# A hybrid conv and gated-linear-attention block: the transposes of the normalized x made by the DMA queue

## The chip, the cores and the metric

The kernel runs on the 8 cores of one Trainium2 chip. Each core has 4,096 of the 32,768 tokens (two of the 16 sequences of 2,048) and does the same work on them; the cores don't speak to each other. The metric is the device time of the slowest core in microseconds (us), as the median of several runs.

## The reference, cut to what matters

x is (16, 2048, 1024) in float32. One layer is computed:

```python
h = rms_norm(x, norm_g)
proj = h @ w_in                      # 1024 -> 8208 columns
c_val, c_gate, c_z, q, k, v, g_lr, g_r, m_conv, m_gla = split(proj)
y_conv = conformer_conv_branch(c_val, c_gate, c_z, ...)   # GLU, 31 taps over positions, LayerNorm, two silu, @ w_conv_out
log_a = log_sigmoid(g_lr @ gate_w2 + gate_b) / 16
o = gla_chunked(q, k, v, log_a)      # causal gated linear attention, 4 heads
y_gla = (rms_norm(o) * silu(g_r)) @ w_gla_out
y = sigmoid(m_conv) * y_conv + sigmoid(m_gla) * y_gla
out = rms_norm(x + y @ w_out)
```

What the change touches is h: every projection multiplies the transpose of h, so h, computed with tokens on the partitions, has to be turned so that its 1,024 channels lie on the partitions.

## The kernel before, in words

**Tiles.** A core's tokens are cut into 8 tiles of 512 (t = 0 to 7), and a tile into 4 slices of 128 tokens (s = 0 to 3). `tile(t)` (line 833) runs the stages of one tile: the GLU units, v, the convolution, q and k, the gates, the attention with the z and m projections as filler, and then an end stage: a loop over c = 0 to 7 (line 940) of three weight units each (g_wco line 916, g_mg line 923, g_wgo line 930), and `wout` (line 792). A unit is a block of 128 x 1024 weights and 8 matmuls of 128x512 on TensorE, 1.73 us.

**The normalized x.** In the end stage of tile t the x of tile t + 1 is made ready, slice by slice. `pre_load` (line 427) loads 128 tokens of x into xa, one of two buffers. `pre_elem` (line 433) squares and sums them on ScalarE (line 440, whose full output is thrown away into hb), takes the inverse root on GpSimd (lines 443 and 446) and writes the scaled slice in bf16 into hb on VectorE (line 449). hb too has two buffers, p = s % 2. `pre_pe` (line 454) transposes the slice: eight 128x128 transposes on TensorE (line 458) from hb into the PSUM bank pb6, and one ScalarE copy (line 461) from pb6 into hT, which holds the transposed tile and has two buffers (hbuf = t % 2). For tile 0 this runs ahead of the first tile, with x in U1. For the others the loop at line 940 calls pre_pe of slice c - 2 at c = 2 to 5, pre_elem of slice c at c = 0 to 3 right behind it, and pre_load of slices 2 and 3 at c = 0 and 1; slices 0 and 1 are loaded in the stage ahead (line 908). The first reader of the new hT is `gate_in(t + 1)` (line 578), at the start of `wout`; it waits for all four slices.

**The order.** Every operation is recorded by `S.op` (line 64) in program order, with the buffers that it reads and writes. Each engine runs its own list in that order; waits between engines come from the buffers, and an engine stands still at a wait with all that is behind it. A write to a buffer waits for the buffer's last write and for its readers. A DMA that SyncE (SP) issues counts as the reader or writer until it has landed. hT[hbuf] is one buffer for all four slices.

**The weights.** All weights pass through SBUF once for each tile. In the first three tiles they come in float32 (512 KB a unit, line 329) into one of 5 staging buffers, are cast to bf16 by VectorE or ScalarE in turn (lines 352 and 355), and a third of them is written back to the DRAM tensor w_b at a time (line 364): tile 0 takes all in float32, tile 1 two thirds, tile 2 one third. The rest, and everything from tile 3 on, is loaded in bf16 from w_b (256 KB a unit, line 345). `advance` (line 367) records these casts and loads ahead of each unit: casts for the next 4 units (LOOK), loads for as many as there are buffers for: 12 units until tile 3, then 22 (NX). All these DMAs are issued by SP, as are those of x, of the result and of the convolution's shifted rows.

Of the kernel before, what the change touches and what calls it, by code (L numbers as in the profile page):

```python
# [148 lines left out]
def build_nc(n_tiles=NT):  # L149
# [13 lines left out]
    S = Sched()  # L163
    dma_sem_names = []

    def newsem(name):
        dma_sem_names.append(name)
        return name

    with ExitStack() as es:  # L170
        def sb(name, shape, dt):
            return es.enter_context(nc.sbuf_tensor("sb_" + name, shape, dt))
# [17 lines left out]
        hb = sb("hb", [128, 2, D], BF16)  # L190
        hT = sb("hT", [128, 2, 8, T], BF16)
# [34 lines left out]
        B = {}  # L226
# [38 lines left out]
        def x0_load(s):  # L265
# [8 lines left out]
             dma_sem=newsem("c_gn"))  # L274
        for s_ in range(1, 4):
# [12 lines left out]
             reads=[B["scanm"]], writes=[B["scanm"]])  # L288
# [126 lines left out]
        def proj_from(t, uid, src, srcbufs, perk=False):  # L415
# [6 lines left out]
                    reads=[wbuf] + ([srcbufs[kc]] if perk else list(srcbufs)), writes=[PB[bi]])  # L422
            return bi

        xa_sems = [newsem("xa0"), newsem("xa1")]

        def pre_load(t, s):
# [26 lines left out]
        def pre_pe(t, s):  # L454
            p = s % 2
            hbuf = t % 2
            for c in range(8):
                S.op("pe", lambda e, p=p, c=c: e.transpose(
                    out=pb6[:, c * 128:(c + 1) * 128], in_=hb[:, p, c * 128:(c + 1) * 128], identity=identb[:]),
                    reads=[B["hb"][p], B["identb"]], writes=[PB[6]])  # L460
            S.op("act", lambda e, hbuf=hbuf, s=s: e.activation(
                out=hT[:, hbuf, :, s * 128:(s + 1) * 128],
                in_=pb6[:].rearrange("p (c t) -> p c t", c=8), func=AF.Copy),
                reads=[PB[6]], writes=[B["hT"][hbuf]])
# [368 lines left out]
        def tile(t):  # L833
# [106 lines left out]
            for c in range(8):  # L940
                g_wco(c)
                g_mg(c)
                if c == 0:
                    gla_c(t, 3)
                else:
                    g_wgo(c - 1)
                if more:
                    if 2 <= c < 6:
                        pre_pe(t + 1, c - 2)
                    if c < 4:  # L950
                        pre_elem(t + 1, c)
                    if c in (0, 1):
                        pre_load(t + 1, c + 2)
# [6 lines left out]
        for s_ in range(4):  # L960
            pre_elem(0, s_)
            if s_ > 0:
                pre_pe(0, s_ - 1)
        pre_pe(0, 3)
        set_pbanks([0, 1, 2, 3, 4, 5, 7])
        gate_in(0)
# [103 lines left out]
```

How the kernel before makes its waits and increments, by code:

```python
    def replay(self, eng, engobj, eng_sems, dma_sems):  # L135
        for o in self.prog[eng]:
            for k, v in o.waits:
                if k[0] == "e":
                    engobj.wait_ge(eng_sems[k[1]], self.cnts[k[1]][v])
                else:
                    engobj.wait_ge(dma_sems[k[1]], v)
            if o.fn is None:
                continue
            inst = o.fn(engobj)
            if o.dma_sem is not None:
                inst.then_inc(dma_sems[o.dma_sem], 16)
            elif o.marked:
                inst.then_inc(eng_sems[eng], 1)
```

## Time and profile before

| | |
|---|---|
| median of 3 runs | 1612.04 us (1610.75 to 1613.39) |
| the profiled execution | 1609.87 us |
| its span, slowest core (core 7) | 1608.3 us |
| spans of the 8 cores | 1592.6 to 1608.3 us |
| TensorE matmul busy | 1478.3 us, 92% |
| VectorE, ScalarE, GpSimd busy | 890.8, 705.4, 555.2 us |
| DMA engines busy with the main hardware queue | 71.5% of 16 engines' span |
| DMA traffic | 352.29 MB, mean 219 GB/s |

Times are those of core 7, from the first instruction to the last. PE is TensorE's matmul side, PEld its weight loads, DVE VectorE, ACT ScalarE, POOL GpSimd, SPq the DMA instructions that SyncE issues. L458 is line 458 of the kernel. In a row of grouped instructions "x8" counts them, and square brackets tell how long the engine had been idle before, and what it waited for. The granted clock (PEclk) is 1.00 at full speed.

### The profile page before, as it was taken

The page shows a single profiled execution, that of the slowest core. Times are in us where ns is not written, and L with a number is a line of the kernel's source. Part 1 is how long each engine was busy: PE and PEld are TensorE (multiplying, and loading weights), DVE is VectorE, ACT ScalarE, POOL GpSimd, SP SyncE. Part 2 cuts the span into 40 slices and gives each one's busy share as a digit, 9 for nine tenths or more (in the row PEclk, how much of TensorE's full clock was granted, in tenths as well). Part 3 has the DMA queues.
Part 4 walks back from the last instruction along what each step waited for, and adds up shares of the span by engine and source line. Part 5 has one row for each costly group of instructions (what it writes and reads, how often), then busy time and mean ns, then how long its engine had stood idle before and what let it go on. Part 6 is the DMA issues. An engine that isn't in the chain of part 4 may idle for free.

```text
span 1608.3 us, 28736 instructions; the slowest of 8 cores (1592.6 to 1608.3 us)
## 1 busy us (share of the span) xinstructions
PE 1478.3 (92%) x8960; PEld 703.2 (44%) x8960; DVE 890.8 (55%) x1259; ACT 705.4 (44%) x1184; POOL 555.2 (35%) x659
## 2 busy tenths in 40 slices
PE   4687989688999899999999999999999999999997
PEld 1233533234544345444554445444544445444553
DVE  3466645475545665476634665376644675366633
ACT  4235755226644256433644245233644246332631
POOL 1123223224223342254423452353423352352512
PEclk9898999889999999999999999999999999999999
DMA  6987899976899868898464955568564856568451
GB/s 184 292 235 222 274 314 318 291 231 200 269 322 286 255 205 252 268 268 243 153 220 143 247 177 184 177 192 242 151 223 145 229 188 200 178 180 241 134 175 53
DMA packets 174820, 352.29 MB, mean 219 GB/s; under 512 B 19536, under 2 KB 60624, under 8 KB 174672
## 3 DMA queue, kind: packets, MB, share of 16 engines
q1 hardware_dynamic: 174528, 350.32, 71.5%
q8 instruction: 76, 1.25, 0.3%
q14 instruction: 72, 0.59, 0.1%
q0 software_dynamic: 144, 0.13, 0.1%
HBM read 301.75 MB, written 48.76 MB: 218 GB/s over the span
## 4 chain that ended last, share of the span: by engine, by line
PE 73%; DMA 10%; DVE 7%; issue 4%; ACT 3%; SPq 2%; POOL 1%; DVEq 0%; POOLq 0%; ACTq 0%
PE ps_pb L409 33%; PE ps_pb L645 13%; PE ps_pb L419 11%; PE ps_pb L795 6%; PE ps_pb L507 4%; DMA sb_stg<-w 4%; DMA usc<-sb_u 3%; DVE sb_U L513 1%; DVE sb_FP L520 1%; SPq L498 1%; DMA w_b<-sb_wn 1%; ACT sb_wn L355 1%; PE ps_pb L707 1%; PE ps_pb L703 1%; PE ps_pb L712 1%
## 5 line engine op out<-in xcount | busy, mean ns | idle before, releaser
L409 PE MATMUL ps_pb<-sb_hT,sb_wn 128*128 128x512 bf16 x2152 | 492.7, 383 | 16.1 <-ACT sb_wn L355 6.9
L409 PEld LDWEIGHTS ps_pb<-sb_hT,sb_wn 128*128 128x128 bf16 x2152 | 209.8, 99 | 271.2 <-issue 38.2
L645 PE MATMUL ps_pb<-sb_wn,sb_hT 128*128 128x512 bf16 x768 | 191.6, 408 | 53.1 <-ACT sb_wn L355 33.1
L409 PE MATMUL ps_pb<-sb_hT,sb_stg 128*128 128x512 bf16 x920 | 207.0, 379 | 1.2 <-issue 0.8
L419 PE MATMUL ps_pb<-sb_big,sb_wn 128*128 128x512 bf16 x744 | 174.7, 382 | 0.4 <-DVE sb_wn L352 0.4
L936 POOL TENSOR_TENSOR sb_yb<-sb_FP 128x512 bf16<-128x512 f32 x64 | 82.7, 1293 | 213.0 <-DVE sb_FP L933 213.0
L645 PEld LDWEIGHTS ps_pb<-sb_wn,sb_hT 128*128 128x128 bf16 x768 | 77.6, 103 | 163.0 <-issue 87.0
L409 PEld LDWEIGHTS ps_pb<-sb_hT,sb_stg 128*128 128x128 bf16 x920 | 89.4, 98 | 105.4 <-issue 2.6
L355 ACT ACTIVATE sb_wn<-sb_stg 128x1024 bf16<-128x1024 f32 x88 | 92.3, 1050 | 98.3 <-DMA sb_stg<-w 98.1
L674 POOL TENSOR_SCALAR sb_Rbf<-sb_Tst,sb_gar 128x256 bf16<-128x256 f32 x128 | 65.7, 531 | 190.8 <-DVE sb_Tst L718 190.7
L522 POOL TENSOR_TENSOR sb_FP<-sb_FP,sb_yb 128x512 f32<-128x512 f32 x56 | 73.8, 1319 | 157.0 <-ACT sb_yb L516 157.0
L555 POOL TENSOR_TENSOR sb_U<-sb_U,sb_FP 128x512 f32<-128x512 f32 x64 | 97.1, 1544 | 57.3 <-DVE sb_FP L541 57.3
L419 PEld LDWEIGHTS ps_pb<-sb_big,sb_wn 128*128 128x128 bf16 x744 | 72.1, 99 | 83.7 <-issue 4.3
L352 DVE CAST sb_wn<-sb_stg 128x1024 bf16<-128x1024 f32 x89 | 68.5, 776 | 63.6 <-DMA sb_stg<-w 63.5
L926 ACT ACTIVATE sb_FP<-ps_pb 128x512 f32<-128x512 f32 x64 | 38.0, 594 | 137.0 <-PE ps_pb L409 116.9
L489 POOL COPY sb_halo<-sb_u 128x30 bf16<-128x30 bf16 x64 | 50.9, 796 | 127.4 <-DVE sb_u L486 127.4
L449 DVE SCALAR_TENSOR_TENSOR sb_hb<-sb_xa,sb_ssx,sb_Gn 128x1024 bf16<-128x1024 f32 x28 | 36.0, 1284 | 102.2 <-POOL sb_ssx L446 102.2
L481 ACT ACTIVATE sb_FP<-ps_pb 128x512 f32<-128x512 f32 x64 | 38.1, 595 | 121.2 <-PE ps_pb L409 80.1
L795 PE MATMUL ps_pb<-sb_wn,sb_yb 128*128 128x512 bf16 x384 | 86.5, 379 | 4.8 <-ACT sb_wn L355 1.8
L740 DVE SCALAR_TENSOR_TENSOR sb_big<-ps_pb,sb_sso,sb_sgr 128x256 bf16<-128x256 f32 x128 | 61.9, 483 | 45.5 <-POOL sb_sso L732 35.5
L507 PE MATMUL ps_pb<-sb_big,sb_wn 128*32 128x512 bf16 x1472 | 80.7, 379 | 2.6 <-issue 2.6
L558 DVE TENSOR_TENSOR sb_U<-sb_U,sb_FP 128x512 f32<-128x512 f32 x64 | 71.1, 1136 | 18.6 <-ACT sb_FP L551 18.6
(115 smaller groups left out, 2083.0 us busy)
## 6 DMA issues: line engine op xcount, KB each, us to landing
sb_stg<-w SPq DMA_DIRECT2D x177, 512.0 KB, 7.7
sb_wn<-w_b SPq DMA_DIRECT2D x329, 256.0 KB, 4.5
sb_stg<-w_b SPq DMA_DIRECT2D x198, 256.0 KB, 3.8
sb_big<-usc SPq DMA_DIRECT2D x256, 135.0 KB, 4.8
w_b<-sb_wn SPq DMA_DIRECT2D x88, 256.0 KB, 6.6
sb_U<-x SPq DMA_DIRECT2D x36, 512.0 KB, 6.6
out<-sb_U SPq DMA_DIRECT2D x32, 512.0 KB, 4.0
sb_xa<-x SPq DMA_DIRECT2D x28, 512.0 KB, 5.4
```

The costliest lines, as they stand in the source:

```text
L352: S.op("dve", lambda e: e.tensor_copy(out=wn[:, slot, :], in_=stg[:, i, :]), reads=[B["stg"][i]], writes=[B["wn"][slot]])
L355: S.op("act", lambda e: e.activation(out=wn[:, slot, :], in_=stg[:, i, :], func=AF.Copy), reads=[B["stg"][i]], writes=[B["wn"][slot]])
L409: S.op("pe", lambda e, bi=bi, kc=kc, wap=wap: e.matmul(pb[bi][:], lhsT=wap[:, kc * 128:(kc + 1) * 128], rhs=hT[:, hbuf, kc, :], start=(kc ...
L419: S.op("pe", lambda e, bi=bi, kc=kc, wap=wap: e.matmul(pb[bi][:], lhsT=wap[:, kc * 128:(kc + 1) * 128], rhs=src[:, kc, :], start=(kc == 0) ...
L507: S.op("pe", lambda e, cbk=cbk, j=j, b=b, c=c, wap=wap: e.matmul(pb[cbk][32 * b:32 * b + 32, :], lhsT=wap[:, b * 256 + j * 32:b * 256 + j ...
L522: S.op("pool", lambda e: e.tensor_tensor(out=FP[:, S2, :], in0=FP[:, S2, :], in1=sq, op=ALU.add), reads=[B["FP"][S2]] + sqbuf, writes=[B[" ...
L555: S.op("pool", lambda e, c=c: e.tensor_tensor(out=U1[:, c, :], in0=U1[:, c, :], in1=FP[:, MU, :], op=ALU.subtract), reads=[B["U1"][c], B[" ...
L558: S.op("dve", lambda e, c=c: e.tensor_tensor(out=U1[:, c, :], in0=U1[:, c, :], in1=FP[:, RS, :], op=ALU.mult), reads=[B["U1"][c], B["FP"][ ...
L645: S.op("pe", lambda e, bi=bi, kc=kc, s=s, wap=wap: e.matmul(pb[bi][:], lhsT=hT[:, hbuf, kc, s * 128:(s + 1) * 128], rhs=wap[:, (kc % 2) * ...
L674: S.op("pool", lambda e, p=p, h=h, s=s: e.tensor_scalar(out=Rbf[:, p, h, :], in0=Tst[:, h, :], scalar1=gar[:, h, s:s + 1], scalar2=1.0, op ...
L795: S.op("pe", lambda e: e.matmul(pb[bi][:], lhsT=yb[:, kc, s * 128:(s + 1) * 128], rhs=wap[:, (kc % 2) * 512:(kc % 2) * 512 + 512], start=( ...
L936: S.op("pool", lambda e, c=c, t1=t1, g2=g2: e.tensor_tensor(out=yb[:, c, :], in0=FP[:, t1, :], in1=FP[:, g2, :], op=ALU.add), reads=[B["FP ...
```

## The change

From the second tile on (t > 0), a slice is transposed by one DMA that SP issues from hb straight into hT. The eight transposes on TensorE, their PSUM bank and ScalarE's copy are left out for these slices. Tile 0 is as before. The two semaphores are one for each hb buffer. The DMA reads hb[p] and writes hT[hbuf] by the bookkeeping of `S.op`.

```diff
+        ht_sems = [newsem("ht0"), newsem("ht1")]
         xa_sems = [newsem("xa0"), newsem("xa1")]
...
         def pre_pe(t, s):
             p = s % 2
             hbuf = t % 2
+            if t > 0:
+                S.op("sp", lambda e: e.dma_start_transpose(out=hT[:, hbuf, :, s * 128:(s + 1) * 128], in_=hb[:, p, :]),
+                     reads=[B["hb"][p]], writes=[B["hT"][hbuf]], dma_sem=ht_sems[p])
+                return
             for c in range(8):
```

## Rows read from the trace of the kernel before

**Rows 1.** The page: busy time of the engines, granted clock and DMA by slices

```profile
PE 1478.3 (92%) x8960; PEld 703.2 (44%) x8960; DVE 890.8 (55%) x1259; ACT 705.4 (44%) x1184; POOL 555.2 (35%) x659
...
PEclk9898999889999999999999999999999999999999
DMA  6987899976899868898464955568564856568451
```

**Rows 2.** The page: the chain that ended last, by engine

```profile
PE 73%; DMA 10%; DVE 7%; issue 4%; ACT 3%; SPq 2%; POOL 1%; DVEq 0%; POOLq 0%; ACTq 0%
```

**Rows 3.** Busy time by stretches: span, PE, PEld, DVE, ACT, POOL, clock, DMA share, GB/s

```profile
200.00:600.00 400.00, 349.90 (x2045) 160.00 (x2044) 221.55 (x304) 184.72 (x278) 128.36 (x146) 0.94 0.87 270
600.00:1608.00 1008.00, 984.77 (x6051) 478.31 (x6049) 564.80 (x798) 425.00 (x758) 375.18 (x441) 1.00 0.64 195
195.00:300.00 105.00, 91.84 (x446) 41.03 (x446) 53.15 (x72) 50.48 (x67) 29.32 (x39) 0.98 0.98 310
300.00:340.00 40.00, 26.58 (x190) 10.87 (x194) 17.36 (x23) 10.28 (x12) 5.02 (x5) 0.74 0.98 280
340.00:400.00 60.00, 51.95 (x331) 23.17 (x324) 39.09 (x53) 30.23 (x48) 26.82 (x24) 0.89 0.63 209
420.00:480.00 60.00, 56.95 (x300) 26.76 (x298) 25.45 (x39) 30.37 (x48) 15.25 (x18) 0.97 1.00 321
640.00:676.00 36.00, 35.45 (x195) 16.75 (x193) 15.60 (x22) 13.37 (x19) 11.67 (x14) 1.00 0.94 309
```

**Rows 4.** Waits of PE before 640 us: what for, us in total, times, longest

```profile
PE ps_pb L645 <- ACT sb_wn L355: 33.1, 12, 5.4
PE ps_pb L458 <- DVE sb_hb L449: 18.0, 3, 15.1
PE ps_pb L645 <- DVE sb_wn L352: 16.5, 7, 7.6
```

**Rows 5.** Timeline of PE in the end stage of tile 6

```profile
1374.99 0.61 PE L458 MATMUL ps_pb<-sb_identb,sb_hb 128*128 128x128 bf16 x8
1375.44 1.89 PE L419 MATMUL ps_pb<-sb_big,sb_wn 128*128 128x512 bf16 x8
1377.17 1.89 PE L409 MATMUL ps_pb<-sb_hT,sb_wn 128*128 128x512 bf16 x8
...
1391.87 0.61 PE L458 MATMUL ps_pb<-sb_identb,sb_hb 128*128 128x128 bf16 x8
1392.32 1.89 PE L419 MATMUL ps_pb<-sb_big,sb_stg 128*128 128x512 bf16 x8
...
1404.89 0.61 PE L584 MATMUL ps_pb<-sb_hT,sb_wglr 128*32 128x512 bf16 x8 [0.32 <-issue]
```

**Rows 6.** All instructions of line 461, with who waited for them

```profile
L461 ACT ACTIVATE sb_hT<-ps_pb x32: 1005/1023/1024, 16.2 to 1392.6; 128x1024 bf16<-128x1024 bf16 x32
...
  PE ps_pb L458: 3.0, 1
```

**Rows 7.** Timeline of ScalarE, VectorE and SP in the end stage of tile 6

```profile
1376.62 1.05 ACT L440 ACTIVATE sb_hb<-sb_xa 128x1024 bf16<-128x1024 f32 x1
1378.92 1.28 DVE L449 SCALAR_TENSOR_TENSOR sb_hb<-sb_xa,sb_ssx,sb_Gn 128x1024 bf16<-128x1024 f32 x1 [2.87 <-POOL sb_ssx L446]
1380.12 0.68 DVE L919 SCALAR_TENSOR_TENSOR sb_FP<-sb_yb,ps_pb 128x512 f32<-128x512 bf16 x1
...
1374.93 0.33 SPq L430 DMA_DIRECT2D sb_xa<-x  x1
1375.31 8.05 SPq L345 DMA_DIRECT2D sb_wn<-w_b  x8
```

**Rows 8.** DMA issues in 1368 to 1405 us: KB each, median us to landing

```profile
sb_wn<-w_b SPq DMA_DIRECT2D x13, 256.0 KB, 5.1
sb_stg<-w_b SPq DMA_DIRECT2D x10, 256.0 KB, 2.7
```

**Rows 9.** Timeline of SP and ScalarE in the end stage of tile 1

```profile
442.02 0.33 SPq L430 DMA_DIRECT2D sb_xa<-x  x1
...
445.11 6.73 SPq L329 DMA_DIRECT2D sb_stg<-w  x2
451.89 0.50 SPq L364 DMA_DIRECT2D w_b<-sb_wn  x1
...
447.24 1.06 ACT L440 ACTIVATE sb_hb<-sb_xa 128x1024 bf16<-128x1024 f32 x1 [4.02 <-DMA sb_xa<-x]
448.20 0.19 ACT L440 ACTIVATION_READ_ACCUMULATOR sb_hb<-sb_xa 128x1 f32 x1
448.51 1.06 ACT L355 ACTIVATE sb_wn<-sb_stg 128x1024 bf16<-128x1024 f32 x1
```

**Rows 10.** DMA issues in 420 to 470 us

```profile
sb_stg<-w SPq DMA_DIRECT2D x17, 512.0 KB, 11.0
w_b<-sb_wn SPq DMA_DIRECT2D x8, 256.0 KB, 10.7
```

**Rows 11.** The page: the main DMA queue's packets, MB, share of 16 engines

```profile
q1 hardware_dynamic: 174528, 350.32, 71.5%
```

## The prediction

> **What bounds the kernel now.** I read the page first. TensorE is busy 92% of the span [rows 1] and makes 73% of the chain that ended last, DMA 10% [rows 2]. These are averages over two regimes, so I cut the span into stretches. From 600 us on PE is busy 984.8 of 1008 us at full clock, with DMA at 0.64; from 200 to 600 us it is busy 349.9 of 400, with DMA at 0.87 [rows 3]. Up to tile 2 the weights come in float32, and there DMA is the bound: 0.98 from 195 to 340 us and 1.00 from 420 to 480, just where the end stages of tiles 0 and 1, and their transposes, lie [rows 3]. PE pays with waits for casts, 33.1 us for ScalarE's and 16.5 for VectorE's [rows 4]; the clock drops too, to 0.74 in the stretch where PE is most idle [rows 3]. In the end stages from tile 2 on PE is the bound: its groups follow each other without a gap [rows 5]. So the change touches two kinds of places: two slow boundaries (from tile 0 to 1 and 1 to 2, 8 slices) bound by DMA and casts, and five boundaries (20 slices) bound by PE.
>
> **What it removes.** From one group of eight transposes to the next matmul is 1375.44 - 1374.99 = 0.45 us, though the group's row says 0.61, as matmuls overlap [rows 5]. The last slice's group is alike, 1392.32 - 1391.87 [rows 5]; all 28 slices make 12.6 us. In the five PE-bound boundaries nothing else stands beside them, so 20 x 0.45 = **9.0 us** come off. In the other two, TensorE's 3.6 us lie in front of waits for weights: I count nothing. ScalarE's copy, 1.02 us x 28 = 29 us [rows 6], is no gain of its own where ScalarE has room; PE waited for it once, 3.0 us [rows 6], in the first boundary. I leave that as a bonus inside the range.
>
> **What it adds, on the DMA engines.** The kernel has no transposing DMA, so I bound it. Low end: 256 KB at the queue's mean rate while busy, 350.32 MB / (0.715 x 1608.3 us) = 305 GB/s, 0.86 us on all 16 engines [rows 11]. High end: a 128x128 block of bf16 has source rows of 256 bytes; if each of the 1,024 is a packet and costs as much as the mean packet now, 0.715 x 16 x 1608.3 us / 174528 = 105 ns [rows 11], a slice costs 1,024 x 105 / 16 ns = 6.7 us. A small packet should cost less than one of 2 KB, so I stay near the low end, at twice it, 1.7 us. A boundary then adds 6.8 us of DMA work. At the slow boundaries, with a share of 0.98 to 1.00, it goes on the path whole; at the others it is hidden, with 0.64 used and 22 units of weights (38 us) loaded ahead. It can't be below nothing, since no transfer is removed.
>
> The Trainium skill disagrees with itself here, and no row shows the DMA's side. Its page Advanced Engine Details and Errata (X-Bar Transpose) says that transposing DMAs are as fast as regular ones, which is my low end; by that an estimate of the sum is some 5 us lower, 1620. Its page VectorE: DVE Perf Modes (The three transpose paths) speaks against the change: 1309 ns for a 128x128 block by DMA, 390 on TensorE. Eight blocks one after another would be, as an estimate, 10.5 us a slice, beyond my high end, and the result that of rival (D) or above. For TensorE the trace differs from that page, with 0.45 us for all eight in a row.
>
> **What it adds, in waits.** Three are new. (1) hb has two buffers, and ScalarE's square of slice 2 writes into the one that slice 0's DMA reads. It stands right behind the DMA in the program, so ScalarE stands still until that has landed; likewise slices 3 and 1. Before, it waited for 0.45 us of TensorE. (2) The four DMAs write one buffer, so SP stands at each until the last has landed, its weight loads behind it. (3) SP waits for hb, which is written two iterations earlier and is ready. The issue itself, 0.33 us for a plain DMA [rows 7], could take longer; one or two us of it on SP are covered by the loads ahead.
>
> In the PE-bound boundaries: SP reaches slice 0's DMA after three loads from 1375.31, at about 1376.4 [rows 7]; it lands L later. From the start of a square to hb it is now 1378.92 + 1.28 - 1376.62 = 3.6 us, and 0.7 more for the VectorE operation behind it that empties a bank [rows 7]. The seven PSUM banks come round after 7 x 1.73 = 12.1 us, for the unit that starts at 1375.44 at 1387.5 [rows 5]. So PE is not held if 1376.4 + L + 4.3 is below 1387.5, L below 6.8 us. Landings of 256 KB here are 2.7 and 5.1 us [rows 8]. The last slice lands at some 1397, and gate_in starts at 1404.9 now [rows 5]. I price both waits at nothing here; the cover is those 2 to 4 us.
>
> In the slow boundaries a DMA of 256 KB lands after 10.7 us [rows 10]. SP reaches slice 0's DMA between 445 and 452 us, so it lands at 456 to 463, and the square that ran at 447.24, with the cast at 448.51 behind it, comes 9 to 16 us later [rows 9]. Casts are recorded only 4 units (7 us) ahead, so PE runs dry for 2 to 9 us, and slice 1's DMA, issued only when slice 0's has landed, does it again. DMA works on meanwhile through its full staging buffers, so this is not added whole to its 6.8 us: between 6.8 (all covered) and 17 (6.8 and two stalls of 5) I take 10 for each boundary, **20 us** in all. The boundary from tile 2 to 3 has DMA at 0.94 [rows 3] but a third of the casts: I take 2 us.
>
> **Sum.** -9.0 + 20 + 2 = +13. Against the profiled execution's 1609.9 us that is 1623; its time lies 2.2 us under the median of the runs, 1612.0, so I forecast 1625 us. About 0.2% (3 us) can be told from no change.
>
> **Rivals.**
> (A) *Hidden everywhere, faster.* The DMAs cost little and land soon, the staging buffers ride over ScalarE's stop, and only the 9 us (at best 12.6 and the 3.0) remain: 1603 us. For it: slices 2 and 3 of x land late anyway, and ScalarE already stood 4.02 us there [rows 9]; DMA has room behind the stage, 0.63 from 340 to 400 us [rows 3]. Against it: 0.98 to 1.00 in between. Chance 0.30.
> (B) *It cancels.* The slow boundaries lose 4 to 5 us each, DMA work at the low end and a short stop: 1612. Chance 0.10.
> (C) *My forecast,* slower by ScalarE's stop behind the queued DMA in tiles 0 and 1: 1625, own range 1616 to 1650. Chance 0.48.
> (D) *Long transposes, much slower.* At the high end, 6.7 us each, the slow boundaries add 54 us of DMA; with landings of 10 us in the wide tiles PE is held 3 us at each of five: -9 + 54 + 15 = +60, and some more for the stops, about 1680. It decides from L above 6.8 us. Chance 0.10.
> (E) *Not what it says:* if elements went one by one, or the DMA were cut into many, SP or the queue would be blocked for far longer, beyond 1700. Chance 0.02; nothing in the profile bears on it.
>
> **Range and chances.** The range runs from the centre of (A) over (B) to the end of (C), 1603 to 1650, and leaves out (D), (E) and the better side of (A), about 0.2. Faster is (A), 0.30; same is (B), 0.10; slower are (C), (D) and (E), 0.60.
>
> **What would show it.** Line 458 has 32 transposes in place of 256, line 461 4 copies, both before tile 0; between units of the end stage from tile 3 on nothing, and each of these stages 1.8 us shorter. A DMA row of 28 with a landing: under 6.8 us in late tiles and near 10 in tiles 0 and 1. Line 440 waiting for that DMA (what reads hb), most in tiles 0 and 1, and PE's waits for ACT L355 above 33.1 us. SP waiting at the second to fourth of each four. I am wrong if the stretch up to 600 us is not longer, or if the wide tiles show gaps on PE in the end stage, or if gate_in waits for the DMA.

## The result, and the profile after

The changed kernel takes 1645.38 us (median) against 1612.04 before: ratio 1.0195, 95% interval 1.0147 to 1.0243. It is slower, by 33 us where 13 were forecast. In some executions, of most of these kernels, the cores of one die show a lower granted clock and the time is some per cent longer; the ratios are taken without them. The profiled execution of the changed kernel has a span of 1643.9 us on core 4, the slowest. The page, in the lines that answer to [rows 1], [rows 2] and [rows 11]:

```profile
PE 1469.4 (89%) x8608; PEld 693.2 (42%) x8736; DVE 890.1 (54%) x1259; ACT 677.5 (41%) x1156; POOL 555.5 (34%) x659
...
PE 67%; DMA 11%; DVE 8%; issue 5%; ACT 3%; SPq 3%; POOL 2%; DVEq 0%; POOLq 0%; ACTq 0%
...
q1 hardware_dynamic: 204096, 357.67, 73.1%
```

And all instructions of line 459, the new DMA: durations on SP in ns (least, median, most), who waited for them (us, times), and the time to landing:

```profile
L459 SPq DMA_TRANSPOSE sb_hT<-sb_hb x28: 1237/1239/6661, 220.9 to 1429.4; - x28
...
  ACT sb_hb L441: 103.9, 14
...
DMA to landing us min/median/max: 3.1/5.5/11.0
```

There are 28 transposing DMAs, as said. Each brings (204096 - 174528) / 28 = 1,056 packets: the source's 1,024 runs of 256 bytes and little else. The queue's busy time went from 0.715 x 1608.3 to 0.731 x 1643.9 us, 51.8 us more, 1.85 us a slice on all 16 engines (1.7 was taken). These are two single cores; by the medians of the 8 cores it is 1.5 us. ScalarE waited 103.9 us for them, in 14 waits, two at each of seven boundaries. PE waited for one at the start of gate_in, once and for 0.4 us.

The stretches, in the columns of [rows 3], the last two cut out of stalls in the end stages of tiles 0 and 1:

```profile
200.00:600.00 400.00, 320.29 (x1792) 142.22 (x1816) 202.53 (x279) 156.80 (x236) 111.74 (x130) 0.90 0.86 257
600.00:1641.00 1041.00, 1003.50 (x5944) 484.03 (x6033) 580.73 (x822) 424.85 (x771) 391.44 (x456) 0.99 0.67 199
220.00:240.00 20.00, 7.40 (x25) 2.85 (x26) 3.68 (x5) 3.02 (x5) 2.00 (x3) 0.66 0.70 176
460.00:480.00 20.00, 8.08 (x26) 2.91 (x25) 3.08 (x4) 2.58 (x4) 2.00 (x3) 0.66 0.74 216
```

From 200 to 600 us PE is busy 320 us in place of 350. In the stalls the DMA share is 0.70 and 0.74, where it was 0.97 and 1.00 in the same stretches before: SP issues no loads for 8.3 us of the first one, as it waits for the cast on VectorE. The granted clock is 0.66 on average there, so it was for a part at 1.2 GHz, the lower of its two levels (full speed is 2.4), after PE had been idle for some 12 us.

The best measure is the time from one gate_in to the next, read from the timeline of each core. Medians over the 8 cores, of the profiled executions; the first column holds the boundary from tile 0 to 1:

```
                               0>1    1>2    2>3    3>4    4>5    5>6    6>7
before                       223.3  220.4  201.6  182.5  182.5  182.5  182.5
the changed kernel           235.6  235.0  213.5  180.8  181.3  180.7  180.8
e1 four hb                   225.1  221.0  203.1  181.1  180.7  181.0  180.8
e2 square elsewhere          232.3  230.2  209.7  182.1  181.8  180.7  180.8
e3 plain copy                238.6  235.2  215.1  181.7  181.2  181.1  181.4
e4 from tile 4               223.5  220.5  202.6  180.8  180.9  180.9  180.7
e5 four hb, four hT          222.9  221.2  202.2  181.1  181.2  181.4  181.1
e6 one step earlier          221.8  222.5  203.5  180.7  180.7  180.7  180.8
e7 twice, late               220.4  218.3  201.5  187.7  188.2  187.2  188.8
e8 four hb, TensorE          219.9  218.8  201.4  182.5  182.5  182.5  182.5
e9 one step earlier, again   223.6  224.1  202.1  180.7  180.7  180.7  180.8
e10 four buffers, from 3     221.2  221.0  200.4  181.3  181.4  181.2  181.0
e11 twice, early             242.6  237.1  218.2  182.2  180.7  181.0  180.8
e12 second aside             230.3  227.8  208.4  182.6  180.7  181.0  180.8
```

The changed kernel loses 12.3, 14.6 and 11.9 us at the first three boundaries and gains 1.2 to 1.8 at each of the last four: +32.4. The first two columns scatter by 2 to 4 us between executions of the same code for these tiles, the last four hardly. The profiled executions of e1 (1622.0 us) and e12 (1640.2 us) lie above the medians of their runs.

The end stage of tile 0: ScalarE, VectorE, PE and SP.

```profile
219.39 1.06 ACT L355 ACTIVATE sb_wn<-sb_stg 128x1024 bf16<-128x1024 f32 x1 [4.42 <-DMA sb_stg<-w]
230.14 1.06 ACT L441 ACTIVATE sb_hb<-sb_xa 128x1024 bf16<-128x1024 f32 x1 [9.70 <-DMA sb_hT<-sb_hb]
231.11 0.19 ACT L441 ACTIVATION_READ_ACCUMULATOR sb_hb<-sb_xa 128x1 f32 x1
231.20 1.04 ACT L355 ACTIVATE sb_wn<-sb_stg 128x1024 bf16<-128x1024 f32 x1
...
232.46 1.28 DVE L450 SCALAR_TENSOR_TENSOR sb_hb<-sb_xa,sb_ssx,sb_Gn 128x1024 bf16<-128x1024 f32 x1 [15.19 <-POOL sb_ssx L447]
233.66 0.69 DVE L352 CAST sb_wn<-sb_stg 128x1024 bf16<-128x1024 f32 x1
...
220.59 1.89 PE L419 MATMUL ps_pb<-sb_big,sb_wn 128*128 128x512 bf16 x8 [1.89 <-ACT sb_wn L355]
234.49 3.57 PE L409 MATMUL ps_pb<-sb_hT,sb_wn 128*128 128x512 bf16 x8 [12.01 <-DVE sb_wn L352]
...
220.90 4.03 SPq L459 DMA_TRANSPOSE sb_hT<-sb_hb  x1
224.99 1.03 SPq L364 DMA_DIRECT2D w_b<-sb_wn  x1
```

SP issues slice 0's transpose at 220.90, behind a full queue (the share of the DMA engines was 1.0 from 205 to 225 us), and is held 4.03 us by it. The square of slice 2 starts at 230.14, after a wait of 9.70 us, with the cast of an odd unit behind it. PE stands 12.01 us, and not for ScalarE but for *VectorE's* cast of an even unit: VectorE stands in its own order at the scaling of slice 2 (line 450), which needs that square's sum, and its cast comes behind it at 233.66. PE's next unit takes 3.57 us in place of 1.89, at the lower clock. The waits of PE for casts before 640 us, after and then before, to be read beside [rows 4]:

```profile
PE ps_pb L650 <- ACT sb_wn L355: 29.9, 12, 5.1
PE ps_pb L409 <- DVE sb_wn L352: 24.3, 3, 12.0
PE ps_pb L409 <- ACT sb_wn L355: 17.1, 6, 4.3
PE ps_pb L650 <- DVE sb_wn L352: 14.9, 8, 5.5
...
PE ps_pb L409 <- ACT sb_wn L355: 6.9, 4, 2.6
PE ps_pb L409 <- DVE sb_wn L352: 4.9, 5, 2.1
```

The waits in the v and gate stages (line 650) are no longer than before; at line 409 they have grown from 4.9 and 6.9 us to 24.3 and 17.1.

The end stage of tile 6, against [rows 5] and [rows 7]:

```profile
1414.33 1.32 SPq L459 DMA_TRANSPOSE sb_hT<-sb_hb  x1
...
1420.14 1.06 ACT L441 ACTIVATE sb_hb<-sb_xa 128x1024 bf16<-128x1024 f32 x1 [8.31 <-DMA sb_hT<-sb_hb]
...
1419.50 1.89 PE L409 MATMUL ps_pb<-sb_hT,sb_stg 128*128 128x512 bf16 x8
1421.22 3.62 PE L419 MATMUL ps_pb<-sb_big,sb_stg 128*128 128x512 bf16 x15
1424.68 1.89 PE L409 MATMUL ps_pb<-sb_hT,sb_stg 128*128 128x512 bf16 x8
```

Here too ScalarE stands 8.31 us, but PE runs without a gap: issue to landing is 5.8 us, under the 6.8 of the prediction. There are no casts to be late.

### The profile page after: what moved, and what is told of

The parts are those of the page before. It is cut to its first block, busy times and chain, and to the rows that moved or that the text cites. A ratio compares the mean times of both kernels' runs of the same rounds, so it can differ in the third digit from the quotient of the medians.

```text
span 1643.9 us, 28159 instructions; the slowest of 8 cores (1629.1 to 1643.9 us)
## 1 busy us (share of the span) xinstructions
PE 1469.4 (89%) x8608; PEld 693.2 (42%) x8736; DVE 890.1 (54%) x1259; ACT 677.5 (41%) x1156; POOL 555.5 (34%) x659
## 3 DMA queue, kind: packets, MB, share of 16 engines
q1 hardware_dynamic: 204096, 357.67, 73.1%
## 4 chain that ended last, share of the span: by engine, by line
PE 67%; DMA 11%; DVE 8%; issue 5%; ACT 3%; SPq 3%; POOL 2%; DVEq 0%; POOLq 0%; ACTq 0%
PE ps_pb L409 29%; PE ps_pb L650 12%; PE ps_pb L419 10%; PE ps_pb L800 6%; DMA usc<-sb_u 4%; PE ps_pb L512 4%; DMA sb_stg<-w 3%; DMA sb_hT<-sb_hb 3%; DVE sb_U L518 2%; DVE sb_FP L525 2%; SPq L503 1%; DMA w_b<-sb_wn 1%; ACT sb_wn L355 1%; DVE sb_wn L352 1%; DVE sb_HP L532 1%
## 5 line engine op out<-in xcount | busy, mean ns | idle before, releaser
L409 PE MATMUL ps_pb<-sb_hT,sb_wn 128*128 128x512 bf16 x2096 | 485.2, 385 | 48.8 <-DVE sb_wn L352 24.3
L650 PE MATMUL ps_pb<-sb_wn,sb_hT 128*128 128x512 bf16 x756 | 196.1, 416 | 51.0 <-ACT sb_wn L355 29.9
L409 PE MATMUL ps_pb<-sb_hT,sb_stg 128*128 128x512 bf16 x896 | 203.0, 379 | 2.8 <-ACT sb_yb L521 1.7
```

The costliest lines, as they stand in the source:

```text
L409: S.op("pe", lambda e, bi=bi, kc=kc, wap=wap: e.matmul(pb[bi][:], lhsT=wap[:, kc * 128:(kc + 1) * 128], rhs=hT[:, hbuf, kc, :], start=(kc ...
L650: S.op("pe", lambda e, bi=bi, kc=kc, s=s, wap=wap: e.matmul(pb[bi][:], lhsT=hT[:, hbuf, kc, s * 128:(s + 1) * 128], rhs=wap[:, (kc % 2) * ...
```

## The experiments

**Theory W**: the loss is a wait of a buffer's next writer for its reader. Slices 2 and 3 reuse the two hb buffers, and ScalarE and VectorE, which carry the casts, stop behind a DMA that is itself behind a full queue. **Theory Q**: the loss is the work of the DMA engines and of SP. All ratios are to the kernel before.

**e1: four buffers for hb.** Two are hb, two lie in HP, a tile that is idle then.

```diff
+        def hslot(s):
+            if s < 2:
+                return hb[:, s, :], [B["hb"][s]]
+            return (HP[:, 2 * s - 4:2 * s - 2, :].rearrange("p a t -> p (a t)"), B["HP"][2 * s - 4:2 * s - 2])
...
-                out=hb[:, p, :], in_=xs, func=AF.Square, accum_out=ssx[:, col:col + 1]),
+                out=hv, in_=xs, func=AF.Square, accum_out=ssx[:, col:col + 1]),
```

> The changed kernel with four buffers for the normalized slice (two of them in HP, which is idle there), so that neither ScalarE's square nor VectorE's scaling of slices 2 and 3 waits for a DMA transpose. Nothing is left out. Theory W (the loss is the stop of ScalarE and VectorE behind a transpose that is still in the queue): the 40 us of PE waits in the first three boundaries (12.0 + 4.3, 11.9 + 3.4, 4.3 + 4.5) vanish, and 1645 falls to between 1603 (the 9 us saved on PE, and the DMA work hidden) and 1618 (1.85 us of DMA work for each of 8 slices on the path). Theory Q (the loss is DMA and SP time: 1.85 us on 16 engines and 1.2 to 6.7 us of a held SP for each slice): still above 1635, with the same waits of PE for casts.

Measured: 1608.8 us, ratio 0.9967 (0.9936 to 0.9999). It is in W's range. On core 0, the same place as above; line 447 is the square, line 466 the transpose:

```profile
219.79 3.63 SPq L466 DMA_TRANSPOSE sb_hT<-sb_hb  x1
...
218.27 1.06 ACT L355 ACTIVATE sb_wn<-sb_stg 128x1024 bf16<-128x1024 f32 x1 [4.56 <-DMA sb_stg<-w]
219.24 1.04 ACT L447 ACTIVATE sb_HP<-sb_xa 128x1024 bf16<-128x1024 f32 x1
...
223.57 1.89 PE L409 MATMUL ps_pb<-sb_hT,sb_wn 128*128 128x512 bf16 x8 [0.70 <-DVE sb_wn L352]
...
PE ps_pb L596 <- DMA sb_hT<-sb_HP: 4.9, 3, 3.5
```

The same DMA, issued in the same way and holding SP for 3.63 us, costs PE almost nothing here: the square runs at once, and PE's 12.01 us are 0.70. All waits of PE for casts come to 61 us before, 98 in the changed kernel and 60 here (medians of the 8 cores). The three boundaries are 1.8, 0.6 and 1.5 us over those before, with all the DMA work still there. A new wait shows in the last line: gate_in (line 596) stands for the last transposes, 2.6 to 6.6 us in all on each core. That is about the size of what is left over.

**e2: only ScalarE freed.** The square's output, which nobody reads, goes elsewhere.

```diff
-                out=hb[:, p, :], in_=xs, func=AF.Square, accum_out=ssx[:, col:col + 1]),
+                out=HP[:, 0:2, :].rearrange("p a t -> p (a t)"), in_=xs, func=AF.Square, accum_out=ssx[:, col:col + 1]),
```

> The changed kernel, with the full output of ScalarE's square, which nobody reads, written into HP in place of hb. ScalarE no longer waits for a transpose; VectorE's scaling of slices 2 and 3 still does. Nothing of the result is left out. Theory W with ScalarE as the engine that matters: most of the 33 us go, 1615 to 1625. Theory W with either engine enough (VectorE carries half of the casts, and it stands at the same buffer): PE waits for VectorE's casts instead, 1635 to 1645. Theory Q: no difference, 1645.

Measured: 1632.4 us, ratio 1.0117 (1.0084 to 1.0149). 13 of the 36.6 us between the changed kernel and e1 come back, and 24 stay with VectorE's stop alone. The opposite, VectorE free and ScalarE not, was not run. It is between the two forms of W, nearer the second. The wait has moved over:

```profile
DVE sb_hb L450 <- DMA sb_hT<-sb_hb: 79.3, 9, 13.5
```

**e3: a plain DMA of the same runs.** It leaves the transposition out.

```diff
-                S.op("sp", lambda e: e.dma_start_transpose(out=hT[:, hbuf, :, s * 128:(s + 1) * 128], in_=hb[:, p, :]),
+                S.op("sp", lambda e: e.dma_start(out=hT[:, hbuf, :, s * 128:(s + 1) * 128], in_=hb[:, p, :].rearrange("p (c t) -> p c t", c=8)),
```

> The changed kernel, with a plain DMA of the same bytes and the same runs of 256 bytes in place of each transposing one; the transposition is left out. Theory W: what counts is when it lands behind a full queue (10 us), not that it transposes: 1635 to 1650. Theory Q in the form that the transposing kind is the trouble (it holds SP for 1.24 to 6.7 us): below 1625, with landings under 8 us in tiles 0 and 1.

Measured: 1649.3 us, ratio 1.0218 (1.0179 to 1.0256), and by its trace:

```profile
L459 SPq DMA_DIRECT2D sb_hT<-sb_hb x28: 605/606/1098, 223.9 to 1433.1; - x28
...
DMA to landing us min/median/max: 3.1/5.2/10.1
```

That the DMA transposes has no part in the loss, and neither has the time that it holds SP: here that is 1.10 us at most.

**e4: DMA transposes for tiles 4 to 7 only.**

```diff
-            if t > 0:
+            if t > 3:
```

> The change only where TensorE is the bound: DMA transposes for tiles 4 to 7, TensorE's for the first four. Nothing is left out. Both theories: the loss sits in the first three boundaries, and the last four give 1.8 us each (182.6 to 180.8 us from gate_in to gate_in): 1612.0 - 7.2 = 1604.8, between 1603 and 1607. If the early boundaries were not the place, it would stay above 1612.

Measured: 1605.7 us, ratio 0.9959 (0.9934 to 0.9984): as forecast, and 0.4% faster than the kernel before.

**e5: hT too as four buffers**, with e1's; a buffer and a semaphore for each slice, and readers wait for all four.

```diff
-        ht_sems = [newsem("ht0"), newsem("ht1")]
+        ht_sems = [newsem("ht%d" % i) for i in range(4)]
...
-                     reads=hvb, writes=[B["hT"][hbuf]], dma_sem=ht_sems[p])
+                     reads=hvb, writes=[B["hT"][hbuf][s]], dma_sem=ht_sems[s])
```

> The kernel of the four hb buffers, and besides hT kept as a buffer for each slice with a semaphore for each, so that SP no longer waits at a transpose for the one before it (41 us of SP's waits with the four hb buffers). Nothing is left out. Theory W: SP's wait was covered by weights loaded ahead, so no difference beyond the noise: 1603 to 1610. Rival (SP's stop holds up the staging loads in the first three boundaries and is what keeps them 1 to 3 us longer than before): 3 to 6 us faster than with four hb buffers, about 1604, with those boundaries at or under the ones before.

Measured: 1607.2 us, ratio 0.9970 (0.9951 to 0.9988). Against e1's 1608.8 no difference that these intervals can tell. SP's waits for an earlier transpose (41.0 us in e1) are gone, so they were covered; the waits at gate_in stay, 2.0 to 5.4 us on each core.

**e6 and e9: each transpose one step earlier**, with two hb buffers; the same kernel twice.

```diff
-                    if 2 <= c < 6:
-                        pre_pe(t + 1, c - 2)
+                    if 1 <= c < 5:
+                        pre_pe(t + 1, c - 1)
```

> The changed kernel with its two hb buffers, and each transpose recorded one step of the loop earlier (slice c - 1 at c = 1 to 4), 5.2 us ahead of the square that has to wait for it. SP stands at that place for the slice anyway, because of x's next load. Nothing is left out. Theory W: each stop of ScalarE gets some 5 us shorter, and with 4.5 to 12 us of PE waits behind it about half of the 42 us lost in three boundaries comes back: 1618 to 1630. Theory Q: the DMA and SP work is the same, 1645.

> The kernel with each transpose one step of the loop earlier, once more, since its four times lay between 1609 and 1664 while its profile had 1607. By that profile the three early boundaries are within 2 us of the ones before and the four late ones give 1.8 us each: 1605 to 1611. If the profile was a lucky run and half of the loss is still there: 1618 to 1630.

Measured: e6 has no verdict. Two of its four times (1640.5 and 1664.4) are of the kind that the ratios leave out, and the other two are 1608.8 and 1610.9. e9 gave 1612.8, ratio 1.0014 (0.9996 to 1.0031), above its expectation of 1605 to 1611. Both profiles show the early boundaries within 4 us of those before, so far more than the expected half came back. The waits of ScalarE for the transposes fell from 103.9 to 60.8 us in e6, and PE's for casts from 98 to 70, where the kernel before has 61. That a stop shorter by 5.2 us mostly stays inside what casts 4 units ahead cover fits this; no run tests it by itself.

**e7: each late slice twice**, in e4's kernel: the same instruction recorded again, so that the second waits for the first.

```diff
+                S.op("sp", lambda e: e.dma_start_transpose(out=hT[:, hbuf, :, s * 128:(s + 1) * 128], in_=hb[:, p, :]),
+                     reads=[B["hb"][p]], writes=[B["hT"][hbuf]], dma_sem=ht_sems[p])
```

> DMA transposes for tiles 4 to 7 only, each slice done twice, the second after the first has landed: landing of the pair some 9.5 to 10 us after the issue in place of 5.8. A test of the slack of 6.8 us that the seven PSUM banks were said to give. If that is right, PE is held some 3 us for slice 0, and up to as much again for slice 1, in each of four boundaries: 1605.7 + 12 to 24 = 1618 to 1630. If ScalarE's and VectorE's stop has more cover than that (or none was needed): 1605 to 1609.

Measured: 1634.3 us, ratio 1.0147 (1.0107 to 1.0186), above the range. The last boundary on core 5:

```profile
1392.78 1.45 SPq L459 DMA_TRANSPOSE sb_hT<-sb_hb  x1
1398.31 1.22 SPq L461 DMA_TRANSPOSE sb_hT<-sb_hb  x1
...
1401.48 1.06 ACT L441 ACTIVATE sb_hb<-sb_xa 128x1024 bf16<-128x1024 f32 x1 [11.19 <-DMA sb_hT<-sb_hb]
...
1405.82 1.89 PE L409 MATMUL ps_pb<-sb_hT,sb_stg 128*128 128x512 bf16 x8 [2.52 <-DVE sb_FP L926]
...
1415.18 3.37 PE L409 MATMUL ps_pb<-sb_hT,sb_stg 128*128 128x512 bf16 x8 [4.02 <-DVE sb_FP L926]
```

The pair lands after 1401.48 - 1392.78 = 8.7 us, 1.9 over the slack of 6.8, and PE is held 2.52 us at a unit whose PSUM bank has not been emptied. So the slack is real and about of the computed size, and a late tile has only 1 us of it left at 5.8. Slice 1 holds PE for more, 4.02 us, where the expectation had at most 3, and the unit after takes 3.37 us in place of 1.89, which it had left out.

**e8: four hb buffers with TensorE's transposes** (e1's edit on the kernel before).

> The kernel of before (TensorE's transposes throughout) with the four hb buffers: does the new buffer alone move the time? PE waited once for ScalarE's copy and never long for hb in a late tile, so all theories: within 0.2% of 1612. If it were faster by 3 us or more, the gain of the four-buffer kernel would not be the transposes'.

Measured: 1611.8 us, ratio 1.0006 (0.9980 to 1.0032). The buffers alone give nothing.

**e10: e5 with DMA transposes from tile 3 on** (`if t > 2:`).

> Four hb buffers, hT kept slice by slice, and DMA transposes for tiles 3 to 7 only: the version that should be best, with the DMA work left out of the two boundaries bound by DMA. Five boundaries at 1.8 us: 1603.5, between 1601 and 1607. If the boundary from tile 2 to 3 takes the DMA work on its path, 1605 to 1609.

Measured: 1601.9 us, ratio 0.9947 (0.9926 to 0.9968). It is the best median, by its ratio 8.5 us under the kernel before, and 43 under the change as made; its interval overlaps e4's and e5's.

**e11 and e12: the price of more DMA work.** Both are e1 with a second transpose for each slice of tiles 1 to 3. In e11 it repeats the first into hT and so waits for it; in e12 it goes into a tile that nobody reads.

```diff
+                if t <= 3:
+                    S.op("sp", lambda e: e.dma_start_transpose(out=hx[:], in_=hv),
+                         reads=hvb, writes=[B["hx"]], dma_sem=hx_sems[p])
```

> The four-buffer kernel, with each slice of tiles 1 to 3 transposed twice, one after the other: the price of the DMA work alone (1.85 us on 16 engines a slice, 7.4 a boundary) where nobody waits for a hb buffer. If DMA work is on the path whole there, as the prediction's sum had it: 3 x 7.4 = 22 us slower than 1608.8, about 1631. If the queue has room for it: under 1614.

> As the run before, but the second transpose of each slice of tiles 1 to 3 goes into a tile that nobody reads, so that SP doesn't wait between the two. It tells apart the two things that the run before doubled at once. If what cost its 53 us was SP standing still with the staging loads behind it: most of that goes, and what is left is the DMA work alone, between 1609 (hidden) and 1631 (3 x 7.4 us, on the path whole). If it was the DMA work after all (queueing of small packets): still above 1640.

Measured: e11 1661.7 us, ratio 1.0316 (1.0298 to 1.0334); e12 1626.9 us, ratio 1.0111 (1.0067 to 1.0154). In e11 SP stands at the second until the first has landed, here on core 6; lines 466 and 469 are the two, and the last two lines are PE's waits at gate_in in e11 and e12:

```profile
224.91 3.94 SPq L466 DMA_TRANSPOSE sb_hT<-sb_hb  x1
234.43 1.23 SPq L469 DMA_TRANSPOSE sb_hT<-sb_hb  x1
...
242.71 1.06 ACT L355 ACTIVATE sb_wn<-sb_stg 128x1024 bf16<-128x1024 f32 x1 [8.33 <-DMA sb_stg<-w]
...
PE ps_pb L599 <- DMA sb_hT<-sb_HP: 26.2, 3, 14.9
PE ps_pb L601 <- DMA sb_hT<-sb_HP: 15.0, 2, 7.9
```

From 228.85 to 234.43 SP issues nothing, and the cast afterwards waits 8.33 us for staged weights. Of 53 us over e1, 35 belong to that standing, by the difference to e12. The other 18 are the price of 12 more DMAs (23 by the ratios, as the two were measured in different sessions), for which the engines' time alone (12 x 1.85) would be 22; SP's time in issuing them is in it too. But neither price is staging loads or engine time alone. A transpose delayed makes the next one late, and the last one holds gate_in: PE waits there for 3.2 us in e1, 13.6 in e12 and 28.4 in e11 (medians of the 8 cores). So about 10 of e12's 18 us, and 15 of the 35 more in e11, stand at gate_in. The expectations of both runs had left this path out.

## Why the prediction was right, and where its sizes were off

**The direction and the mechanism** were right. The stop at hb (wait 1) is what costs: e1 takes it away and nothing else, and 36.6 us come back. The size was not: +33 for +13. The time still lies in the range because that reached to 1650, and not because its terms were right.

**The late boundaries** came out nearly as said: no gap on PE, and a landing of 5.8 us under the slack of 6.8 (e7 shows that the slack is one). For 1.8 us each the table has 1.2 to 1.8 at four of them; the fifth, from tile 2 to 3, was no such boundary.

**The slow boundaries** were sized at 10 us each and cost 12.3 and 14.6. The step that failed was that only ScalarE's stop was priced. "PE runs dry for 2 to 9 us" took the odd units' casts; VectorE stands at the same buffer with the even ones, and 24 of the 36.6 us stay when ScalarE alone is free (e2). PE stood 12.01 and 11.9 us for VectorE's casts, beyond that range.

**The boundary from tile 2 to 3** was the worst term: 2 us, less 1.8 saved, against a measured 11.9. I reasoned that a third of the casts means a third of the trouble. Here ScalarE and VectorE still stop for a landing, and one cast behind the stop is enough to stop PE: 4.3 us for ScalarE's and 4.5 for VectorE's in that stage, with the clock at 0.77 from 690 to 710 us, where it was 1.00 before. A share of the work tells nothing of a single late item in order.

**The DMA work** was sized well (1.5 to 1.85 us against 1.7) but put in the wrong place. In e1 it is all there, and three boundaries are together 3.9 us longer than before (9.1 longer than in e8, which has the same buffers and no DMA) where 20 to 22 would be on the path; a share of 0.98 to 1.00 still took in more than half. It does not take as much of a second dose, which costs 18 (e12). What is paid shows for a large part as gate_in waiting for the last transpose, a wait that the prediction priced in the late boundaries only. A busy share is not what one more transfer costs.

**The waits of SP** (2) were rightly priced at nothing for one DMA a slice (e5 against e1), and the rival (A), faster with nothing but the 9 us, comes near what happens once the buffer conflict is gone (e1, e4, e10). On the two pages of the Trainium skill: Advanced Engine Details and Errata (X-Bar Transpose) has transposing DMAs as fast as regular ones. For the landing this case agrees (median 5.5 us against 5.2 for a plain DMA of the same runs, e3); the time on the engines is about 1.7 times the plain one's (1.85 us a slice against 1.07, reckoned in the same way). A mean busy time of 1.85 us for eight blocks, and landings from 3.1 us on, are not eight times the 1309 ns of VectorE: DVE Perf Modes (The three transpose paths); as the time of one block alone no run here tests that figure.

## What to carry to other kernels

Moving an operation from an engine to a DMA queue turns a short hold on its input buffer into the DMA's whole landing time, queue included; so look first at who writes that buffer next, and what stands behind that writer in its order, on every engine that writes it, and then at the first reader of what the DMA writes. Give the buffer as many copies as the landing needs, or issue the DMA earlier, before counting what the engine saves. Where a stage is already bound by the queue, leave the operation on the engine: the same edit that costs 12 to 15 us a boundary there gives 1.2 to 1.8 where TensorE is the bound. With enough buffers what is left to save there is small, some 4 us by e10 against e5, which their intervals don't separate.

## What the runs showed of the hardware

A transposing DMA of 256 KB holds SP for 1.24 us. A plain weight load of 256 KB takes 0.33, and a plain DMA with the transpose's runs of 256 bytes 0.61 (e3). Where the queue is full, the transposing one holds SP for up to 6.66 us (at 457.00, with the DMA engines at a share of 0.99 from 440 to 463 us; 4.03 at 220.90), while e3's plain one never takes more than 1.10. I had allowed for the first and not thought of the second.
